# Key and query products of the cross-attention with stationary tokens, turned in 32x32 blocks

## The reference, cut to what matters

```
def cross_attend(xn, memn, wq, wk, wv, wo):
    q = (xn @ wq).reshape(B, S, XA_HEADS, XA_HEAD_DIM)      # 4 heads of 512
    k = (memn @ wk).reshape(B, M, XA_HEADS, XA_HEAD_DIM)
    v = (memn @ wv).reshape(B, M, XA_HEADS, XA_HEAD_DIM)
    scores = jnp.einsum('bshd,bmhd->bhsm', q, k) * (XA_HEAD_DIM ** -0.5)
    p = jax.nn.softmax(scores, axis=-1)
    o = jnp.einsum('bhsm,bmhd->bshd', p, v)
    return o @ wo
```

## Time and profile before

| | us |
|---|---|
| median of three runs | 1489.17 |
| lowest, highest | 1489.03, 1489.21 |
| the profiled execution | 1489.79 |
| its span in the trace | 1488.0 |

### The profile page before, as it was taken

One profiled execution on the slowest core, in us unless ns is written; L12 is line 12 of the kernel. 1 busy time (PEld: TensorE's weight loads), 2 busy tenths in 40 slices (PEclk: granted clock), 3 DMA queues, 4 the chain that ended last, 5 costly groups with the idle time before them and its releaser, 6 DMA issues.

```text
span 1488.0 us, 22342 instructions
## 1 busy us (share of the span) xinstructions
PE 1478.4 (99%) x7186; PEld 1247.9 (84%) x7186; DVE 1025.6 (69%) x1384; ACT 963.5 (65%) x1477; POOL 2.9 (0%) x9
## 2 busy tenths in 40 slices
PE   9999999999999999999999999999999999999997
PEld 8888888888888888888888888888888888888886
DVE  5756666788888566664665776675857676685696
ACT  6644578745555486554767868586766858576974
POOL 0000000000000000000000000000000000000000
PEclk9999999999999999999999999999999999999999
DMA  9756655565556654445555565556555555656554
GB/s 346 259 193 210 218 180 187 199 200 169 175 175 228 197 184 156 156 153 194 190 184 195 186 201 191 190 188 199 187 197 200 186 194 186 199 188 193 195 197 143
DMA packets 81038, 288.93 MB, mean 194 GB/s; under 512 B 9008, under 2 KB 10544, under 8 KB 80096
## 3 DMA queue, kind: packets, MB, share of 16 engines
q1 hardware_dynamic: 76752, 275.68, 55.8%
q10 hardware_dynamic: 3744, 9.30, 1.8%
q0 software_dynamic: 496, 3.34, 0.6%
HBM read 286.19 MB, written 2.10 MB: 194 GB/s over the span
## 4 chain that ended last, share of the span: by engine, by line
PE 98%; ACT 1%; DVE 0%; issue 0%; DMA 0%; ACTq 0%; DVEq 0%
PE ps L282 98%; ACT whi L583 0%; PE ps L343 0%; DMA hl<-in_first_in 0%; DVE wlo L981 0%; PE ps L444 0%; ACT scr L833 0%; DVE sm_ L1349 0%; PE ps L498 0%; DVE tmp L999 0%; ACT scr L956 0%; ACT vm L971 0%; DVE xres L1499 0%; ACTq L118 0%; ACT whi L624 0%
## 5 line engine op out<-in xcount | busy, mean ns | idle before, releaser
L981 DVE TENSOR_TENSOR wlo<-raw,whi 128x1024 fp32r<-128x1024 f32 x516 | 624.7, 1220 | 314.6 <-ACT whi L583 305.6
L583 ACT ACTIVATE whi<-raw 128x1024 fp32r<-128x1024 f32 x516 | 531.4, 1053 | 222.6 <-PE ps L282 216.2
L282 PE MATMUL ps<-whi,xT 128*128 128x512 f32 x1536 | 475.1, 389 | 0.0
L282 PE MATMUL ps<-whi,mixT 128*128 128x512 f32 x1472 | 457.0, 390 | 0.3 <-ACT whi L624 0.3
L282 PEld LDWEIGHTS ps<-whi,xT 128*128 128x128 f32 x1536 | 288.4, 188 | 59.8
L282 PEld LDWEIGHTS ps<-whi,mixT 128*128 128x128 f32 x1472 | 276.8, 188 | 57.9 <-issue 0.6
L282 PE MATMUL ps<-xT,whi 128*128 128x512 f32 x896 | 310.5, 398 | 0.3
L282 PE MATMUL ps<-wlo,xT 128*128 128x512 f32 x768 | 298.8, 389 | 0.0
L282 PE MATMUL ps<-wlo,mixT 128*128 128x512 f32 x736 | 285.1, 389 | 0.0
L282 PE MATMUL ps<-xT,wlo 128*128 128x256 f32 x896 | 234.9, 278 | 0.0
L282 PEld LDWEIGHTS ps<-xT,whi 128*128 128x128 f32 x896 | 162.8, 188 | 32.2 <-DVE wlo L981 0.9
(11 more groups left out here) (186 smaller groups left out, 744.7 us busy)
## 6 DMA issues: line engine op xcount, KB each, us to landing
raw<-in_stream SPq DMA_DIRECT2D x518, 512.0 KB, 3.3
xres<-in_xin ACTq DMA_DIRECT2D x2, 1024.0 KB, 7.3
scr<-in_xt_in ACTq DMA_DIRECT2D x8, 256.0 KB, 3.6
xres<-in_xin POOLq DMA_DIRECT2D x1, 2048.0 KB, 11.9
out_x<-vm SPq DMA_DIRECT2D x8, 256.0 KB, 3.1
raw<-in_stream SPq DMA_DIRECT2D x4, 256.0 KB, 4.3
kT<-in_memt_in ACTq DMA_DIRECT2D x2, 512.0 KB, 5.7
vbuf<-in_memin ACTq DMA_DIRECT2D x1, 1024.0 KB, 10.0
```

The lines of the kernel that those rows point to most:

```text
L282: return nc.tensor.matmul(o, l, r, start=start, stop=stop, skip_group_check=True)
L583: A(whi[:, 2 * pr + s, :], raw[:, 2 * pr + s, :], ACT.Copy).then_inc(hi_done, 1)
L981: V.tensor_tensor(wlo[:, 2 * pr + s, :], raw[:, 2 * pr + s, :], f32(whi[:, 2 * pr + s, :]), ALU.subtract).then_inc(lo_done, 1)
```

## The change

Both products, `wk` and `wq`, become `wide`. The weights are laid out accordingly, and the removed parts are the half sums, the scaling by `row_mem`, and the small product that made that row (`row_of(0)`). Since the results now have tokens on partitions and the scores need features there, each group of 512 features is turned: kept by ACT as rows (for the keys with the token's scale), transposed in 32x32 blocks by DVE, and moved between partition groups by 16 copies. For the keys all 16 are ACT's, in the four steps that follow the group. For the queries ACT and DVE take 8 each in the group's last step. The loops over rounds and heads are unrolled. `load_x` now waits for `xt_lo`, and `x_hi` and `x_lo` move behind the second split.

The query stage is reordered too. PE runs `scores` of the head before in the third wide product of a head, `probs_tr` in the fourth, and `attend` in the first one of the next head. High and low parts of a query are made in one instruction each per head.

```
-            narrow(C_KM // 2, 0, mixT, {}, 2)
-            narrow(C_KM // 2, 1, mixT)
-            with pe.Fori(1, KT // 2) as i:
-                for pr in range(2):
-                    narrow(C_KM // 2 + i, pr, mixT)
+            for n in range(16):
+                wide(C_KM // 2 + n // 2, n % 2, mixT, range(n % 4 * 4, n % 4 * 4 + 4), (4, 2, 4, 0)[n // 4], n % 4 == 0, n % 4 == 3)
...
-            for j in range(4):
-                narrow(C_Q // 2 + j // 2, j % 2, xT, {} if j else NEXT, 0 if j else 8)
-            with pe.Fori(1, XH) as h:
-                for j in range(4):
-                    narrow(C_Q // 2 + 2 * h + j // 2, j % 2, xT, {(10, 12, 10)[j]: lambda: [ATT[j](h), 3][1]} if j < 3 else {})
+            for h in range(XH):
+                for n in range(4):
+                    mid = None
+                    if h == 0:
+                        pe.wait_ge(nt_lo, 4 * n + 4)
+                        mid = (lambda: norm_tr(3)) if n == 0 else None
+                    elif n == 0 and h > 1:
+                        mid = lambda: attend(h - 1)
+                    elif n > 1:
+                        mid = lambda: (scores, probs_tr)[n - 2](h)
+                    wide(C_Q // 2 + 2 * h + n // 2, n % 2, xT, range(4 * n, 4 * n + 4), Q_BANKS[h], n == 0, n == 3, mid)
...
+                    if half == 0 and n == 0:
+                        mid = lambda: attend(XH - 1)
+                    elif half == 0 and 2 <= n < 5:
+                        mid = lambda: (scores, probs_tr, attend)[n - 2](XH)
...
+            def load_x(i):
+                if i:
+                    act.wait_ge(xt_lo, 2 * i)
+                act.dma_start(xstage, xt_in[:, 2 * i:2 * i + 2, :]).then_inc(x_in, 16)
...
+            for h in range(XH):
                 m = C_Q // 2 + 2 * h
...
+                step(m, 0, (lambda: out_and_query(h)) if h else None)
+                step(m, 1, None, (lambda: take_values(h)) if h else None)
+                step(m + 1, 0, (lambda: scaled_exps(h)) if h else lambda: keys_hi(0))
+                step(m + 1, 1, lambda: last_probs_and_rows(h), lambda: move_query(h, 0), lambda: move_query(h, 1))
...
+            for n in range(16):
+                step(C_KM // 2 + n // 2, n % 2, None, (lambda: turn_keys(n // 4)) if n % 4 == 3 else None,
+                     (lambda: x_lo(n // 2)) if n % 2 else None)
...
+            for h in range(XH):
+                m = C_Q // 2 + 2 * h
+                step(m, 0, (lambda: out_and_query(h)) if h else q_scale)
+                step(m, 1, None, (lambda: values_lo(h)) if h else None)
+                step(m + 1, 0, (lambda: softmax_max(h - 1)) if h else None, (lambda: norm_and_keys(h)) if h else lambda: keys_lo(0))
+                step(m + 1, 1, lambda: probs_and_blocks(h), lambda: move_query(h, 2), lambda: move_query(h, 3))
```

More of the change, by code:

```diff
@@ L63 @@
 NC = C_F + 2 * NF + NF
-W_KM, W_YU, W_H, W_Q, W_F = 0, 16, 32, 56, 72
+W_YU, W_H, W_Q = 0, 16, 40
 PAN = 1024
@@ L326, in wide, with row_of @@
                         mid()
-            def row_of(n):
-                pe.wait_ge(diag_ready, n + 1)
+            def row_of():
+                pe.wait_ge(diag_ready, 1)
                 for tt in range(TT):
@@ L681, in _, with x_hi, keep_keys, move_keys @@
                 step(n // 2, n % 2, None, side.get(n), side.get((n, 2)))
[L684 to L696, removed]
+            def load_x(i):
+                if i:
+                    act.wait_ge(xt_lo, 2 * i)
+                act.dma_start(xstage, xt_in[:, 2 * i:2 * i + 2, :]).then_inc(x_in, 16)
+            def x_hi(i):
+                act.wait_ge(x_in, 16 * i + 16)
+                hi_tiles(xstage, xT, O_G1, 2 * i, xt_hi)
+            def keep_keys(g):
+                for tt in range(TT):
+                    A(km_rows[:, tt, :], ps[:, (4, 2, 4, 0)[g] + tt, :], ACT.Copy, scale=rcol[:, 0, tt:tt + 1]).then_inc(km_kept, 1)
+            def move_keys(g, i):
+                act.wait_ge(km_turned, 2 * g + 2)
+                for q in range(4):
+                    A(kT[q * 32:(q + 1) * 32, 4 * g:4 * g + 4, :].rearrange("p j (t i b) -> p j t i b", t=TT, i=4)[:, :, :, i, :],
+                      km_blocks[i * 32:(i + 1) * 32, q], ACT.Copy).then_inc(km_moved, 1)
+            for n in range(16):
+                def before_split():
+                    if n % 4 == 3:
+                        keep_keys(n // 4)
+                    elif n % 2 == 0:
+                        load_x(n // 2)
+                def between():
+                    if n >= 4 and n % 4 < 3:
+                        move_keys(n // 4 - 1, n % 4)
+                def behind():
+                    if n % 2:
+                        x_hi(n // 2)
+                    elif n >= 4 and n % 4 == 0:
+                        move_keys(n // 4 - 1, 3)
+                step(C_KM // 2 + n // 2, n % 2, before_split, between, behind)
             act.wait_ge(halves_set, 1)
@@ L1396, in _, with turn_query @@
-            q_head(0, False)
-            ch.enter(0, 2, 1)
-            with dve.Fori(1, XH) as h:
-                ch.reg = h
-                q_head(h, True)
-            ch.leave(XH)
-            wide_norm(C_XO, 4, O_G3, {0: lambda: attend_parts(XH), 2: lambda: out_split(XH)}, {})
+            def turn_query(h):
+                dve.wait_ge(q_kept, 2 * h + 2)
+                if h:
+                    dve.wait_ge(q_moved_act, 8 * h)
+                for tt in range(TT):
+                    V.transpose(q_blocks.rearrange("p q j t b -> p t j q b")[:, tt], q_rows[:, tt, :]).then_inc(q_turned, 1)
@@ new lines, in move_query, with query_lo, probs_and_blocks @@
+            def move_query(h, i):
+                dve.wait_ge(q_turned, 2 * h + 2)
+                for q in range(4):
+                    V.tensor_copy(*q_move(i, q)).then_inc(q_moved_dve, 1)
+            def query_lo(h):
+                dve.wait_ge(q_hi_done, h + 1)
+                V.tensor_tensor(q_lo[:], tmp[:, 0:4, :], f32(q_hi[:]), ALU.subtract).then_inc(qT_ready, 1)
+            def probs_and_blocks(h):
+                if h:
+                    probs_lo(h)
+                turn_query(h)
```

166 lines of the change are left out of this document (82 added, 84 removed).

## The result

The changed kernel is slower, and by more than the range allowed:

| | before | after |
|---|---|---|
| median, us | 1489.14 | 1514.5 |
| executions, us | 1489.03, 1489.12, 1489.17, 1489.21 | 1511.77, 1514.14, 1514.86 |
| profiled execution, us | 1489.79 | 1514.86 |
| its span, us | 1488.0 | 1513.1 |
| ratio after / before | | 1.0163, interval 1.0147 to 1.0179 |

A forecast was written before the change was run, and what follows sets the result against it. PE was taken as the bound (98% of the chain of waits). -1.7 - 2.6 - 0.4 + 14.35 + 0.5 + 0.7 + 3.1 = +13.95 us gave a median of 1503.2 us, own range 1500.5 to 1506, full range 1498.5 to 1508.

The forecast's parts named there:

- PE's own work: Fewer matmuls per panel: -1.7 us in the key stage, -2.6 in the query stage, and -0.4 for a removed product.
- the 0.4 us for `row_of(0)`: Saving of 0.4 us on PE from dropping the small product that made the row.
- The softmax's waits: PE waits at `probs_tr` for normalised probabilities, 4.8, 3.5, 3.5 and 2.55 us in four heads: +14.35 us.
- The query of head 1: After head 0, moves, high and low parts delay a split to near 6.0 where 5.44 is due: +0.5 us once.
- The key stage: ACT's steps run late because `load_x` waits for `x_lo`: PE loses +0.7 us in all.
- a lag of 0.7 us: Delay of PE around the key stage, from ACT starting the steps after chunks 13 and 14 late.
- The bound given, 0 to 2: Range in us stated for the key stage's lag, around +0.7.
- The wait for `xT`: At the start of the `u` and `y` stage PE waits for DVE's last tiles: +3.1 us, between 1.9 and 4.
- the rival on the clock: PE's waits lower its clock, 1.5 to 3 us a fall: one fall 1505 to 1506.5, 14%; more, near 1513 with four, 4%.
- The prediction's last line: Signs of error: maximum under 0.2 us after scores, DVE's copies much over 0.43 us, or granted clock falling after a wait.
- Its other reading: At the kernel's start four matmuls took 1.95 us, read as the pace of 1.2 GHz, 5.5 us into the span.
- The sum: All terms together: +13.95 us on the profiled execution's 1489.8, which is 1503.8 us.

The follow-up runs named there:

- all_three: Changed kernel with softmax a step earlier, `xT` splits between the panel splits, and head 1's query parts between the splits; 1484.84 us, ratio 0.9971 to before.
- fill_short: Changed kernel plus unread dummy matmuls: 4, 3, 3 and 2 ahead of the probabilities' transposes, 3 ahead of the `xT` wait; 1506.97 us, ratio 1.0121.
- the second trace of the changed kernel: Changed kernel run again unmodified, in the same batch as later experiments; median 1512.88 us, ratio 1.0166.
- softmax_early: Changed kernel with each head's whole softmax one step earlier, behind the second split, waiting for the scores alone; 1493.59 us, ratio 1.0028.
- x_early: Changed kernel with both splits of `xT` back between the panel splits, ahead of the key transposes; 1505.88 us, ratio 1.0117.
- fill_wait: Changed kernel plus 9, 6 and 6 unread dummy float32 matmuls ahead of the probabilities' transposes in heads 1 to 3; 1513.7 us.
- query_only: Changed kernel with memory's key product left `narrow`, so only the query stage is changed; 1507.86 us, ratio 1.0121.

## Why the prediction was wrong, point by point

**PE's own work: right.** Without waits it comes out at -2.1 and -2.7 us, with -2.1 and -2.6 predicted. The forecast's saving was read from starts, 13 ns a matmul in the key stage and 2.6 us in the query stage, and both held; the 0.4 us for `row_of(0)` was never measured alone. The Trainium skill ("TensorE: Matmul & The Clock Gate", section "Wait — 56ns, not 53.3ns?") has a fixed cost of 2.5 ns for a matmul, by which both would have been 0.6 us in all; the trace of `all_three`, with 4.7 us, doesn't agree with it.

**The softmax's waits: right.** Predicted 4.8, 3.5, 3.5 and 2.55, measured 4.71, 3.43, 3.44 and 2.49. In the changed kernel the chain reads on DVE and ACT as it was laid out, in this order:

```profile
604.09 0.69 DVE L1385 TENSOR_REDUCE sm_<-ps 128x2 f32<-128x512 f32 x1 [4.22 <-PE ps L295]
...
605.05 1.28 ACT L864 ACT_TABLE_LOAD   x1 [7.43 <-DVE sm_ L1386]
606.35 0.56 ACT L864 ACTIVATE scr<-ps,sm_ 128x256 f32<-128x256 f32 x1
...
607.45 1.05 ACT L875 ACTIVATE k_head<-kT 128x1024 fp32r<-128x1024 f32 x1
608.39 1.99 ACT L588 ACTIVATE whi<-raw 128x1024 fp32r<-128x1024 f32 x2
...
609.47 1.23 DVE L1020 TENSOR_TENSOR wlo<-raw,whi 128x1024 fp32r<-128x1024 f32 x1 [4.50 <-ACT whi L588]
610.62 0.16 DVE L1391 RECIPROCAL sm_<-sm_ 128x2 f32<-128x2 f32 x1
610.81 0.62 DVE L1393 TENSOR_SCALAR scr<-scr,sm_ 128x256 f32<-128x256 f32 x2
```

ACT stands idle for 7.43 us ahead of the table load, which then runs inside the chain, the key copy and a split stand ahead of DVE's split, and the products end when the transposes start. What the sum left out is a small restart: in `fill_short`, which has no falls, query and output stage are 13.1 us longer than before, where -2.6 + 14.35 + 0.5 gives 12.25. That is 0.9 us too little, some 0.2 at each of the four waits. The same is seen without dummies: in the second trace of the changed kernel the transposes at 646.72 and 678.44 are 31.72 us apart, with one wait of 3.43 us and no fall between them, and in `softmax_early`, without the wait, they are 28.09 apart, so that wait cost 3.63.

**The query of head 1: right**, 0.74 us at 595.38 for 0.5. DVE's four copies of 32 x 256 took 1.25 us, 0.31 each, the lower of its two bounds.

**The key stage: mis-sized.** With a lag of 0.7 us the stretch up to 183.84 should have become 1.4 us shorter and became 0.7 longer, so the lag is 2.8 (2.0 by the trace of `fill_short`, whose stretch ends at 183.07); 3.1 came back in `x_early`. The mechanism was named (`load_x` waits for `x_lo` and heads ACT's step), but the reckoning from durations laid end to end had it bite in two steps only. In the trace PE stands in four places (2.3 us that can be seen as gaps in its starts), two of them at 160.75 and 183.84 with 0.7 and 0.8 us. The bound given, 0 to 2, was too low as well, or just reached.

**The wait for `xT`: right**, 2.9 us for 3.1.

**The failed step is the rival on the clock.** The sum put the falls of PE's clock at nothing, and they cost 7.8 us. The rival had the mechanism and the price, "1.5 to 3 us" for a fall, and the runs show 1.2 to 2.7. What failed is the chance. The text read the end of the kernel as "it fell from 2.4 to 1.2 GHz some 5.3 us after" and concluded "The waits of 3.5 to 4.8 us are shorter, but not by much", which made a single instance into a threshold. Even at the kernel's end that instance doesn't repeat. In `all_three` PE's last matmul ends at 1475.62, and the clock falls near 1478.4, 2.8 us later (PE's timeline, then the busy time by stretch):

```profile
1475.23 0.39 PE L295 MATMUL ps<-whi,mixT 128*128 128x512 f32 x1
...
1478.00:1479.00 1.00, 0.00 (x0) 0.00 (x0) 1.00 (x2) 1.00 (x2) 0.00 (x0) 0.72 0.09 33
```

Over all ten traces this distance is between 2.5 us (`fill_short`) and 5.4 us (`fill_wait`), and that of the kernel before was near the longest. In the waits of the changed kernel the clock fell 3.6, 2.1 and 2.0 us after PE had stopped (606.77 to 610.4, 642.43 to 644.5, 676.70 to 678.7). One fall got 14% and more than one 4%, where three was what happened, and three or four falls in each trace of a kernel that keeps all four waits unfilled. The rule quoted from the Trainium skill, that gaps between bursts bring the lower clock back, was the one that the traces bear out; it stood there as a sentence and moved no number. The prediction's last line did name the sign that came, a granted clock that fell after a wait. Its other reading, that the first four matmuls in 1.95 us ran at the pace of 1.2 GHz, isn't borne out by the granted clock, which the profile gives as 1.00 there; what that pace was due to stays open:

```profile
5.00:6.00 1.00, 0.71 (x2) 0.50 (x2) 0.97 (x3) 1.00 (x3) 0.00 (x0) 1.00 0.85 283
6.00:7.00 1.00, 1.00 (x4) 0.74 (x3) 1.00 (x4) 0.83 (x3) 0.00 (x0) 1.00 0.98 365
```

**The sum.** Of the 25.0 us, 7.8 are falls of the clock, 2.1 the key stage, 0.9 the restarts and 0.3 the `u` and `y` stage, beyond the 13.95 predicted. Without falls the profiled execution would be at 1514.86 - 7.8 = 1507.1, inside the range, though above the 1506 that the forecast gave as its own upper end, for the key stage and the restarts; the falls put it outside.

## What to carry to other kernels

A wait of the matmul engine costs more than its length: expect a fall of the clock on top of a wait of 2.5 us and more. Here 15 of 22 had one, at 1.2 to 2.7 us each, so a forecast has to count them, with a range for how many there are. The form of product was a gain from the start, and what lost 28 us was the place of the work of ACT and DVE that stands between two matmuls; the same instructions one step earlier made the kernel faster than the one before. When an instruction is queued behind a wait that it doesn't need (a table load, the first use of a step's buffers, a load at a step's head), it moves into the chain with its whole duration.

## What the runs showed of the hardware

- The clock isn't governed by the length of a wait alone. Waits of 2.8 and 2.9 us had a fall in three of five traces, and of 2.5 us in two of five. In a wait it fell as early as 2.0 us after PE's stop; in 5 of the 15 falls it fell only after PE had started again, by 0.5 us (607.23 to 607.7, in `query_only`) to 1.5 us (702.63 to 704.1, in `x_early`), and so it can't be seen in the wait itself. The last of these in `x_early`, PE's timeline and then the busy time by stretch:

```profile
702.63 0.66 PE L497 MATMUL ps<-ident,scr 128*128 128x128 f32 x4 [2.49 <-DVE scr L1397]
...
700.00:704.00 4.00, 1.51 (x9) 1.25 (x9) 3.05 (x5) 1.54 (x2) 0.00 (x0) 1.00 0.39 133
704.00:706.00 2.00, 2.00 (x6) 1.58 (x6) 0.00 (x0) 0.00 (x0) 0.00 (x0) 0.52 0.82 252
```

- Once down it stayed down for 3.4 or for 6.8 us, though PE was working for most of it. What decides between the two stays open.
- The Trainium skill ("TensorE: Matmul & The Clock Gate", section "Why this matters for your kernels") warns of idle gaps between matmul bursts. The traces agree that the clock falls at them, but show it at gaps shorter than the page warns of: 2.50 us in `query_only` and 2.49 in `x_early`.
- In `fill_wait` a matmul of 512 columns with float32 operands took 0.86 us, 3.8 times the 0.227 us between starts of those with rounded operands.
